# Three softmax attentions of a two-block transformer kernel: alternating heads, values by query tile, strips split in pieces

## What is computed

```
def context_attention(q, k, v):                       # 6 heads of 64, 256 queries, 256 keys
    s = jnp.einsum('bqhd,bkhd->bhqk', q * HEAD_DIM ** -0.5, k)
    p = jax.nn.softmax(s, axis=-1)
    return jnp.einsum('bhqk,bkhd->bqhd', p, v)
# _mla: 8 heads, query and key 64 + 32 (rotated) wide, value 64, 512 queries, 512 keys
# _mem_xattn: 4 heads of 256, 512 queries, 256 keys
```

## Time and profile before

| | us |
|---|---|
| three runs | 2754.55, 2757.94, 2771.48 |
| median | 2757.94 |
| profiled execution | 2757.81 |
| its span in the profile | 2756.0 |
| TensorE busy in the span | 2482.0 (90%) |
| VectorE busy | 1347.5 (49%) |
| ScalarE busy | 863.8 (31%) |
| GpSimd busy | 285.0 (10%) |
| mean granted TensorE clock | 0.954 of full speed |

### The profile page before, as it was taken

How to read it: one execution, slowest core, us unless ns; L and a number is a source line. 1 busy time by engine, 2 the same in 40 slices (tenths; PEclk the granted TensorE clock), 3 DMA queues, 4 the chain that set the end, 5 groups by cost and what they waited for, 6 DMA issues and landing times. The chain is left out here.

```text
span 2756.0 us, 34813 instructions
## 1 busy us (share of the span) xinstructions
PE 2482.0 (90%) x14602; PEld 1933.4 (70%) x14602; DVE 1347.5 (49%) x2163; ACT 863.8 (31%) x1379; POOL 285.0 (10%) x229
## 2 busy tenths in 40 slices
PE   7998889999998998998889999998977789898976
PEld 5887558888887888996669998865733368583322
DVE  3323554566667213324647777356575655423213
ACT  3223443332224113224443433233414542310001
POOL 0401420000000000302400000000042020011112
PEclk9999989999999999998999999999998999988999
DMA  5115731111111112126412223320201014348997
GB/s 242 62 54 127 257 112 46 57 67 62 62 62 32 59 60 80 62 69 204 154 62 84 92 91 141 94 72 31 88 0 55 0 62 140 120 197 331 421 420 292
DMA packets 58411, 325.32 MB, mean 118 GB/s; under 512 B 8269, under 2 KB 14541, under 8 KB 26317
## 3 DMA queue, kind: packets, MB, share of 16 engines
q1 hardware_dynamic: 47390, 303.30, 30.4%
q0 software_dynamic: 5696, 12.59, 1.2%
q10 hardware_dynamic: 5168, 7.18, 0.9%
HBM read 315.71 MB, written 12.58 MB: 119 GB/s over the span
## 5 line engine op out<-in xcount | busy, mean ns | idle before, releaser
L955 PE MATMUL ps<-work_rounded,ring_rounded 128*128 128x512 f32 (+1 forms) x2016 | 537.1, 354 | 18.8 <-DVE work_rounded L397 10.3
L955 PE MATMUL ps<-xn_rounded,ring_rounded 128*128 128x512 f32 (+2 forms) x2304 | 542.4, 347 | 0.0
L2007 PE MATMUL ps<-xn_rounded,ring_rounded 128*128 128x258 f32 (+2 forms) x2816 | 534.9, 312 | 0.0
L2007 PEld LDWEIGHTS ps<-xn_rounded,ring_rounded 128*128 128x128 f32 x2816 | 414.8, 191 | 31.3
L955 PEld LDWEIGHTS ps<-xn_rounded,ring_rounded 128*128 128x128 f32 x2304 | 373.8, 191 | 57.5 <-issue 0.2
L955 PEld LDWEIGHTS ps<-work_rounded,ring_rounded 128*128 128x128 f32 x2016 | 336.4, 192 | 75.7 <-DVE work_rounded L397 10.9
L955 PE MATMUL ps<-big_rounded,ring_rounded 128*128 128x512 f32 (+1 forms) x1200 | 325.8, 363 | 45.2 <-DVE big_rounded L861 25.0
L861 DVE TENSOR_TENSOR ring_rounded<-ring,ring_rounded 128x2048 fp32r<-128x2048 f32 (+2 forms) x94 | 190.0, 2025 | 268.7 <-ACT ring_rounded L826 268.7
L2007 PE MATMUL ps<-work_rounded,ring_rounded 128*128 128x256 f32 (+1 forms) x1232 | 280.4, 309 | 9.0 <-PEq L786 4.8
L955 PEld LDWEIGHTS ps<-big_rounded,ring_rounded 128*128 128x128 f32 x1200 | 203.2, 196 | 85.1 <-DVE ring_rounded L861 21.8
L826 ACT ACTIVATE ring_rounded<-ring 128x2048 fp32r<-128x2048 f32 (+2 forms) x94 | 158.1, 1687 | 315.1 <-PE ps L955 292.0
(11 more groups left out here) (415 smaller groups left out, 3048.8 us busy)
## 6 DMA issues: line engine op xcount, KB each, us to landing
ring<-in_stream SPq DMA_DIRECT2D x141, 1024.0 KB, 4.9
big<-in_experts SPq DMA_DIRECT2D x44, 1024.0 KB, 25.9
ring<-in_stream SPq DMA_DIRECT2D x32, 704.0 KB, 4.0
ring<-in_experts SPq DMA_DIRECT2D x22, 1024.0 KB, 27.1
xn<-in_experts SPq DMA_DIRECT2D x15, 1024.0 KB, 28.4
work<-in_experts SPq DMA_DIRECT2D x15, 1024.0 KB, 28.7
big<-in_first_modulation SPq DMA_DIRECT2D x8, 1024.0 KB, 14.3
work<-in_bias ACTq DMA_DIRECT2D x16, 256.0 KB, 6.3
```

Of the source, the lines that this page charges most:

```text
L955: mm = pe.matmul(out[:, a - u.first:b - u.first], lhs, rhs, start=j == 0 and n == 0 and not u.onto, stop=j == terms - 1 and n == len(passe ...
L2007: mm = pe.matmul(out[:, a:b], ws[:, k, :], x[k][:, a - base:b - base], start=k == 0 and n == 0, stop=k == KT - 1 and n == 2)
```

## The change

In attention, for all three calls:

- In the paired calls the units of two heads alternate: unit u of a pair is head 2p + r % 2, query tile r // 2. The memory attention keeps its order.
- Values are multiplied as soon as a group is copied: in the paired calls a group is two units (the same query tile of both heads), in the memory attention one unit. Each product moves 128 columns. The turned tiles now lie in four areas of one unit each.
- The paired calls have two banks for turned scores (4 and 7) and one output bank (6). The memory attention has one and three (5, 6, 7).
- The two strips split ahead are taken in eight pieces of 512 columns. ScalarE makes a high part after units 4, 7, 10, 13, 17, 20, 23, 26 (latent) or 4, 5, 6, 7, 9, 10, 11, 12 (memory), VectorE the low part one unit later.
- The sum of squares runs at the sixth unit of the next pair instead of the fourth of its first head. A one-element Sqrt is added ahead of the last square.

In latent_queries_and_keys the eight copies of the rotated rows move from ScalarE to VectorE, each behind a rotation.

```diff
-        turned_areas = [tmp[:, at + i * nk * nq * P:at + (i + 1) * nk * nq * P] for i in range(2)] + (paired.areas if paired else [])
-        pt = [a.rearrange("p (k q) -> p k q", k=nk) for a in turned_areas]
+        units = heads * nq
+        span = 2 * nq if paired else nq
+        group = 2 if paired else 1
+        pt = [tmp[:, (4 + i) * width:(5 + i) * width].rearrange("p (k q) -> p k q", k=nk) for i in range(4)]
...
-        tpsum = self.ps[:, 2048:2048 + width]
-        opsum = [self.bank(6 + i) for i in range(2)]
+        tpsum = [self.bank(b, width) for b in ((4, 7) if paired else (4,))]
+        opsum = [self.bank(b) for b in ((6,) if paired else (5, 6, 7))]
...
+        strip_pieces = [(n, value[:, a:z], high[:, a:z]) for n, value, high in views for a, z in pieces(value.shape[1])]
+        piece_at = {4 + n * (units - 6) // len(strip_pieces): n for n in range(len(strip_pieces))} if strip_pieces else {}
...
+        def head_and_tile(u):
+            if paired:
+                p, r = divmod(u, span)
+                return 2 * p + r % 2, r // 2
+            return divmod(u, nq)
...
+                def turn(u):
+                    pe.wait_ge(normed.sem, normed.at(u + 1))
+                    if u >= len(tpsum):
+                        pe.wait_ge(copied.sem, copied.at(u - len(tpsum) + 1))
                     for j in range(nk):
+                        mm = pe.transpose(tpsum[u % len(tpsum)][:, j * P:(j + 1) * P], pbuf[u % 4][:, j * P:(j + 1) * P], self.ident)
+                    mm.then_inc(turned.up(), 1)
+
+                def values(g):
+                    members = range(g * group, (g + 1) * group)
+                    pe.wait_ge(copied.sem, copied.at((g + 1) * group))
+                    h, i = head_and_tile(members[0])
+                    for n in range(n_out):
+                        m = h // 2 if paired else h * n_out + n
+                        if i == 0 and m >= len(opsum):
+                            pe.wait_ge(stored.sem, stored.at(m - len(opsum) + 1))
+                        for j in range(nk):
+                            for u in members:
+                                h, _ = head_and_tile(u)
+                                out = opsum[m % len(opsum)][64 * (h % 2):64 * (h % 2) + 64] if paired else opsum[m % len(opsum)]
+                                mm = pe.matmul(out[:, i * P:(i + 1) * P], v(h, j, n), pt[u % 4][:, j, :], start=j == 0, stop=j == nk - 1)
                     mm.then_inc(valued.up(), 1)
...
+                    turn(u)
+                    if u % group == 0 and u >= group:
+                        values(u // group - 1)
+                    if pair_at(u, 5) is not None:
+                        sum_pair(pair_at(u, 5))
...
-                values(heads - 1)
+                values(units // group - 1)
...
+                def store(s):
+                    dve.wait_ge(valued.sem, valued.at((s + 1) * span // group))
                     if paired:
+                        dve.tensor_copy(paired.tile(s), opsum[s % len(opsum)][:, 0:nq * P]).then_inc(stored.up(), 1)
                         return
                     for n in range(n_out):
+                        dve.tensor_copy(outs(s)[n], opsum[(s * n_out + n) % len(opsum)][:, 0:nq * P]).then_inc(stored.up(), 1)
...
-                    if u % nq == min(1, nq - 1) and u >= nq:
-                        store(u // nq - 1)
-                    if u == 5:
-                        self.low_ahead(dve, views)
+                    if u % span == 1 and u >= span:
+                        store(u // span - 1)
+                    if u - 1 in piece_at:
+                        n = piece_at[u - 1]
+                        dve.wait_ge(piece_high.sem, piece_high.at(n + 1))
+                        self.split_low(dve, *strip_pieces[n][1:])
...
+                def copy(u):
+                    act.wait_ge(turned.sem, turned.at(u + 1))
+                    if u >= 4:
+                        act.wait_ge(valued.sem, valued.at((u - 4) // group + 1))
+                    act.activation(pt[u % 4], tpsum[u % len(tpsum)].rearrange("p (k q) -> p k q", k=nk), ACT.Copy).then_inc(copied.up(), 1)
...
-                    if u == 4:
-                        self.high_ahead(act, views)
+                    if u in piece_at:
+                        n, value, high = strip_pieces[piece_at[u]]
+                        act.wait_ge(self.landed[n % RING], 16 * (n // RING + 1))
+                        self.split_high(act, value, high).then_inc(piece_high.up(), 1)
...
                 if normed_pairs:
+                    act.activation(stat[:, 2, 0:1], stat[:, 2, 0:1], ACT.Sqrt)
                     square_pair(heads // 2 - 1)
...
-                    if n >= 12:
-                        if n == 12:
-                            act.wait_ge(rotated.sem, rotated.at(1))
-                        act.activation(kk[64:96, n - 12, :], p2[64:96, MKR, :], ACT.Copy)
...
                     dve.tensor_tensor(tile, tile, sines[s % 2], ALU.add).then_inc(rotated.up(), 1)
+                    if s >= 1:
+                        if s == 1:
+                            dve.wait_ge(rotated.sem, rotated.at(1))
+                        dve.tensor_copy(kk[64:96, s - 1, :], p2[64:96, MKR, :])
```

More of the change, by code:

```diff
@@ L1060, in attention @@
         views = self.split_ahead(ahead)
+        strip_pieces = [(n, value[:, a:z], high[:, a:z]) for n, value, high in views for a, z in pieces(value.shape[1])]
+        piece_at = {4 + n * (units - 6) // len(strip_pieces): n for n in range(len(strip_pieces))} if strip_pieces else {}
+        piece_high = self.sig("strip_high")
         next_high = self.sig("next_high")
+        def head_and_tile(u):
[3 more added lines that the diff above has]
+            return divmod(u, nq)
         def pair_at(u, place):
-            h, i = divmod(u, nq)
-            return h // 2 - 1 if normed_pairs and i == place and h >= 2 and h % 2 == 0 else None
+            p = u // span
+            return p - 1 if normed_pairs and u % span == place and p >= 1 else None
         with self.stage() as block:
@@ L1120, in _ @@
                         modulation.products(pe, n)
-                    pe.wait_ge(normed.sem, normed.at(u + 1))
-                    if u >= 1:
-                        pe.wait_ge(copied.sem, copied.at(u))
-                    for j in range(nk):
-                        mm = pe.transpose(tpsum[:, j * P:(j + 1) * P], pbuf[u % 4][:, j * P:(j + 1) * P], self.ident)
-                    mm.then_inc(turned.up(), 1)
-                    if u % nq == 0 and u >= nq:
-                        values(u // nq - 1)
-                    if pair_at(u, 3) is not None:
-                        sum_pair(pair_at(u, 3))
+                    turn(u)
[3 more added lines that the diff above has]
+                        sum_pair(pair_at(u, 5))
                     for n in share[u][1:2]:
@@ L1186, in _ @@
                             self.split_low(dve, value, high)
-                store(heads - 1)
+                store(units // span - 1)
                 if modulation:
@@ L1211, in _ @@
                         modulation.copy(act, n)
-                    self._turn_copy(act, u, nq, nk, turned, copied, valued, n_out, pt, tpsum)
+                    copy(u)
                     if u + 3 < units:
@@ L1615, in context_attention @@
             modulation=ModulationProducts(self, MOD_CONTEXT, MOD_SECOND - MOD_CONTEXT, self.bank(5), tiles_in(256, self.work[:, 9216:9728])),
-            paired=Paired(lambda p: px[:, NAQ + p, S:T], tiles_in(512, self.work[:, 2048:3072])))
+            paired=Paired(lambda p: px[:, NAQ + p, S:T]))
     def load_ramp(self, sp):
@@ L3073 @@
     tile: object
-    areas: list
 @dataclasses.dataclass
```

46 lines of the change are left out of this document (10 added, 36 removed).

## The result

The changed kernel takes 2740.74 us (median of 11 runs, 2729.69 to 2750.14) against 2757.94 (median of 11 runs, 2749.58 to 2771.63). The ratio is 0.9935 with an interval of 0.9915 to 0.9954: 0.65% less, 17 to 18 us, a little less than the 20.3 us forecast, and within the range. The profiled execution took 2740.90 us, its span 2739.1.

What follows compares the result with a forecast made beforehand. Waits between engines were taken to bound latent and memory attention, the clock the context attention. Latent -11.7, key copies -1.4, memory -6.7 and context -0.5 sum to -20.3: from 2757.8 to 2737.5 us, range 2725 to 2751.

Steps and rivals of the forecast that it cites:

- Values by query tile, 1.03 us: Latent and memory attention: a group of 128-column value products takes TensorE 1.03 us; ends 0.91 and 2.13.
- Rival A: Latent and memory values: weight loads are not covered by running products, adding 35 us, total 2773 us; chance 4%.
- The latent attention: TensorE becomes the bound, 3.89 us per two units plus 8.2 us idle in all; stage shorter by 11.7 us.
- the phase of the extras: Latent attention: extra VectorE work at odd units delays TensorE by its whole length; at even units 0.87 us is spare.
- The memory attention: TensorE needs 2.17 us a unit, with about 3.0 us idle behind stores, pieces and tiles; stage shorter by 6.7 us.
- The key copies: Queries and keys: moving eight rotated-row copies from ScalarE to VectorE saves 1.4 us, or 1.0 by the shared-port rule.
- the second bank: Latent attention: a second bank for turned scores is worth nothing in the steady part and counts only in the tail.
- the Sqrt: Latent tail: the early Sqrt moves its 1.28 us table load beside the last values and store, saving 0.1 us.
- Rival B: Latent and memory attention: VectorE stays the pacer, extras stall TensorE at even units too, +9.6 us, 2747; chance 18%.
- The context attention: No more work and a last value block half as long, -0.5 us; clock effect, -9 to +13, taken as 0.
- Rival C: Extras overlap in the attentions (-8) and the context clock rises with the first values (-3): 2727 us; chance 20%.
- Rival D: Context attention: the clock stays low to the end of the stage, +13 us, total 2750 us; chance 6%.

Runs made afterwards that it cites:

- experiment 3: Changed kernel with VectorE's strip pieces and mixer tiles all at even units of the latent attention, stores still at odd ones: latent stage 77.85 us, against 80.87.
- experiment 4: Changed kernel with all eight strip pieces at odd units of the latent attention, four of them together with a tile: latent stage 84.62 us, against 80.87.
- experiment 8: Changed kernel with one bank for turned scores instead of two in the paired attentions: latent stage 80.98 us, against 80.87.
- experiment 9: Changed kernel without the added one-element Sqrt ahead of the last square: latent stage 80.97 us, against 80.87.
- experiment 1: Kernel before with only the two strips split in eight pieces, order and values as before: latent 86.08, memory 48.34 us; median 2753.27 us, ratio 0.998.
- the filling: Three unused float32 products added on TensorE behind the context attention's first scores: changed kernel 2736.65 us, combined version 2725.68 us; context stage 32.07 us in both.

## Why the prediction came out right

The sum was 2.8 us too large in all, by misses of both signs that partly cancel: +2.6 in the latent attention, -1.1 in the memory attention, +0.8 at the key copies and +0.5 in the context attention.

- **Values by query tile, 1.03 us.** Right in the latent attention to the hundredth. In the memory attention I took 1.03 and it was 0.89: transposes were the wrong neighbour for a product under 128-wide weights. 16 x 0.14 = 2.2 us too dear. Rival A, uncovered weight loads, is out: in the changed kernel the median loads are 137 ns for 64 columns of weights and 192 ns for 128, and both pass unseen beside records that follow each other every 64 and 111 ns (1.03 us / 16, 0.89 / 8). The rule of the Trainium skill that spoke for A ("TensorE: Matmul & The Clock Gate", Part 3) does not describe these products; the measurement decides.
- **The latent attention, -11.7 forecast, -9.1 measured.** The mechanism held, the phase of the extras above all (experiments 3 and 4). A size was off: two steady units were forecast at 3.89 + 0.16 = 4.05 us and are 4.30. A tenth is the start of the values, 0.58 behind the start of the transposes and not 0.48; a tenth is the idle time, 0.27 and not 0.16. From the first transposes to the next stage it was 2207.37 - 2130.88 = 76.5 us against the 74.0 of the sum. All of the 2.5 us lies in the loop: to the transposes of unit 28 it took 2196.85 - 2130.88 = 66.0 us against 63.5, of which 0.9 are gaps (9.1 against 8.2) and 1.3 the later start of thirteen values. The tail took 10.5 as summed.
- **The memory attention, -6.7 forecast, -7.8 measured.** The stalls were named one by one and came: 0.64 for the store (0.5), 0.99 behind piece and tiles (0.8), 0.93 in the tail (1.0). The values alone would have made the stage 2.2 us shorter than the sum, and it was 1.1 shorter. Most of the other 1.1 went into waits that came out longer: the four in the loop are 3.3 us by the profile against 2.9, and a block of values that waits in its middle takes 1.16 us beside the wait, not 0.89. One sign of being wrong was badly put: a wait of the values for a store was listed there, though the sum itself has one of 0.5 us in this attention; it came, and says nothing against the mechanism.
- **The key copies, -1.4 forecast, -0.6 measured.** The failed step is that only one copy behind the last addition was priced. Of the other seven, the last took 1.41 us, held the last rotation behind it and moved the last addition by 0.9 us. The rule that I had put in a sentence aside (the Trainium skill, "SBUF — State Buffer", shared port pair) was the right one to sum by: the trace agrees, as the copy that started 0.55 us into GpSimd's product ended 0.29 us behind it, and the copies away from a product took 0.42. It cost more than the 0.4 us that I gave it, and it struck one copy, not the last two: no GpSimd product runs beside the eighth.
- **Nothing for the second bank, for the wait of the single output bank, and 0.1 for the Sqrt:** right. Experiments 8 and 9 show the first and the last; for the single output bank no values of the latent attention wait for a store in the trace.
- **Rival B** had VectorE as the pacer at even units. The 9.1 us of gaps are VectorE's, but 8.4 of them stand behind extras at odd units; behind an even unit there is none.
- **The context attention.** The profile after has 37.70 us beside 37.66. The clock does not account for the missing 0.5, as its mean is 0.73 in both. The shorter end came: from the start of the last values to the next stage it is 371.60 - 369.54 = 2.06 us against 371.08 - 368.58 = 2.50. But "no more work" was wrong. Eight records of 256 columns take 1.02 us (362.57 to 363.59), and their two halves 0.59 each (357.98 to 358.57), and 1.05 each at the low clock, where the block before took 1.68 mostly at it (352.31 to 353.99); TensorE is busy 0.63 us longer in the same 38 us:

```profile
362.57 1.08 PE L1094 MATMUL ps<-work,xn 128*64 128x256 f32 x8
363.59 0.44 PE L1125 MATMUL ps<-base,work 128*128 128x128 f32 x2
```

```profile
357.98 0.66 PE L1107 MATMUL ps<-work,xn 128*64 128x128 f32 x8
358.57 0.70 PE L1083 MATMUL ps<-big 64*128 64x256 f32 x2
```

```profile
333.00:371.00 38.00, 34.88 (x256) 19.21 (x256) 13.68 (x58) 13.17 (x44) 0.00 (x0) 0.73 0.60 215
```

That both profiles have the same clock here is luck: each is one draw of a stage that takes 32 to 47 us. The guess that the clock rises with the first values was wrong: with them at 345.95 in place of 352.31 it rose no earlier (0.61 over 353 to 355 after, 0.83 before). My bounds of -9 and +13 were wider than the -6 and +9.5 of the twelve profiles, and the spread is one between executions of the same instructions. Whether the new order also shifts it is not shown: all six long stages belong to the new order, but the old one was profiled only twice (37.66 and 31.77). The medians speak against a large shift, as the other three stages give -17.5 us and the medians differ by 17.2. Rivals C and D, as far as they rest on it, mostly describe executions, not the change.

## What to carry to other kernels

When two engines hand units to each other, sum each engine's load, then follow one unit through the loop and ask at which position the bounding engine has slack; extra work of the other is free there and costs its full length elsewhere (77.9 against 84.6 us for the same instructions). Cutting a long piece of work may be worth little by itself (3.9 us in the latent attention, nothing in the memory attention): it pays where the waiting engine has work of its own to put over the cuts. In the memory attention without such work TensorE's clock still fell twice among the gaps that were left (experiment 1), and that ate about 3 us. And read the stages side by side before trusting a total: the even version of experiment 3 has the latent attention 6.8 us shorter than the odd one, yet its one run took 2745.33 us against 2739.74, as it has the context attention at 46.31 against 32.66.

## What was not expected

- The context attention takes 31.6 to 47.1 us with unchanged instructions. The granted clock fell to the low level in every profile, near the head, and what differed was how long it stayed there: from 3.4 us with the filling and about 7 without, to some 41 (0.57 over 333 to 381 with the copies on ScalarE), with TensorE busy for 44.24 of those 48 us. Why it rises early in one execution and late in another no run here shows.
- Eight float32 records of 128 columns under 128-wide weights take 0.89 us, less than eight transposes of the same shape (1.02).
- A VectorE copy of 0.42 us took 1.41 beside a GpSimd product, and GpSimd's product 1.67 us instead of 1.28; that product took 1.68 before as well, without a copy, and in both a VectorE addition was running when it started (2121.20 for 0.69 us before, with the product at 2121.37).
